# Modulation sums in their own banks, a distance table sent by another queue, and multiplications with constants in TensorE's gaps

## The reference

```python
# layer 1
mod = silu(c) @ w_ada + b_ada
shift, scale, gate = split(mod, 3)
h = rms_norm(x, norm_gain) * (1 + scale) + shift
proj = h @ w_in                 # kc, vc, z, gate, k, v, q of two attentions
...                             # a banded attention and one over compressed, selected and windowed keys,
                                # each with a bias that depends on the distance of query and key
x = x + gate * (concat(o_a * silu(z_a), o_b * silu(z_b)) @ w_out)
# layers 2 and 3, i = 0, 1
mod = silu(c2) @ ada_w[i] + ada_b[i]           # six vectors of 1024
a = rmsnorm(h, norm1[i]) * (1 + sc1) + sh1
y = diff_attention(a, ctx, ...) if i == 0 else short_conv(a, ...)
h = h + g1 * y
h = h + g2 * swiglu(rmsnorm(h, norm2[i]) * (1 + sc2) + sh2, w_gate_up[i], w_down[i])
```

## Time and profile before

| | before |
|---|---|
| median of 3 executions | 1742.04 us (1740.34 to 1745.28) |
| span of the profiled execution | 1739.3 us |
| time of the profiled execution beside it | none is given; the span stands for it, 2.7 us below the median |
| PE busy | 1672.8 us, 96% |
| DVE, ACT busy | 975.8 us (56%), 677.8 us (39%) |
| mean granted clock of PE | 0.979 of full speed |

### The profile page before, as it was taken

How to read it: one execution, slowest core, us unless ns; L and a number is a source line. 1 busy time by engine, 2 the same in 40 slices (tenths; PEclk the granted TensorE clock), 3 DMA queues, 4 the chain that set the end, 5 groups by cost and what they waited for, 6 DMA issues and landing times.

```text
span 1739.3 us, 22898 instructions
## 1 busy us (share of the span) xinstructions
PE 1672.8 (96%) x8888; PEld 1393.1 (80%) x8888; DVE 975.8 (56%) x1805; ACT 677.8 (39%) x1413; POOL 61.9 (4%) x120
## 2 busy tenths in 40 slices
PE   4999999999999999999999999999999899999999
PEld 2777777777999999777888888887888788888887
DVE  4667466766777766767555554436555533333332
ACT  3334555564455555554322222223222433333221
POOL 0000000000000000000000000000000000000000
PEclk9899998999999999998999999998999999999999
DMA  8886333313223131222666665442443233333332
GB/s 309 210 244 180 99 96 98 97 25 87 54 55 104 38 110 37 86 73 56 189 179 182 192 178 153 116 122 75 130 124 97 73 97 97 97 97 97 100 113 79
DMA packets 290215, 202.02 MB, mean 116 GB/s; under 512 B 76247, under 2 KB 272072, under 8 KB 289082
## 3 DMA queue, kind: packets, MB, share of 16 engines
q1 hardware_dynamic: 266942, 133.21, 27.5%
q0 software_dynamic: 15536, 56.37, 10.7%
q10 hardware_dynamic: 7628, 10.97, 1.9%
HBM read 197.33 MB, written 5.28 MB: 116 GB/s over the span
## 4 chain that ended last, share of the span: by engine, by line
PE 88%; DVE 6%; ACT 2%; issue 2%; DMA 2%; ACTq 1%; SPq 0%; DVEq 0%
PE PS L864 13%; PE PS L866 13%; PE PS L865 13%; PE PS L848 4%; PE PS L846 4%; PE PS L847 4%; PE PS L1285 3%; PE PS L1287 3%; PE PS L1286 3%; PE PS L1335 2%; PE PS L1094 2%; PE PS L1359 2%; PE PS L1068 2%; PE PS L1347 1%; PE PS L1076 1%
## 5 line engine op out<-in xcount | busy, mean ns | idle before, releaser
L2016 DVE TENSOR_TENSOR WL<-WS,WH 128x512 fp32r<-128x512 f32 x416 | 268.0, 686 | 256.2 <-ACT WH L1508 255.7
L1508 ACT ACTIVATE WH<-WS 128x512 fp32r<-128x512 f32 x416 | 237.7, 621 | 179.1 <-PE PS L848 130.7
L864 PE MATMUL PS<-A3H,WL 128*128 128x512 f32 x672 | 262.9, 391 | 0.1
L866 PE MATMUL PS<-A3H,WH 128*128 128x512 f32 x672 | 261.7, 389 | 0.0
L865 PE MATMUL PS<-A3L,WH 128*128 128x512 f32 x672 | 261.4, 389 | 0.0
L864 PEld LDWEIGHTS PS<-A3H,WL 128*128 128x128 f32 x672 | 126.1, 188 | 30.0 <-issue 4.4
L866 PEld LDWEIGHTS PS<-A3H,WH 128*128 128x128 f32 x672 | 126.1, 188 | 26.4
L865 PEld LDWEIGHTS PS<-A3L,WH 128*128 128x128 f32 x672 | 126.2, 188 | 26.0
L846 PE MATMUL PS<-GH,WL 128*128 128x512 f32 x352 | 137.4, 390 | 0.6 <-DVE WL L2016 0.6
L848 PE MATMUL PS<-GH,WH 128*128 128x512 f32 x352 | 137.0, 389 | 0.0
L847 PE MATMUL PS<-GL,WH 128*128 128x512 f32 x352 | 137.0, 389 | 0.0
(11 more groups left out here) (363 smaller groups left out, 3429.1 us busy)
## 6 DMA issues: line engine op xcount, KB each, us to landing
AW<-in_ada_w POOLq DMA_DIRECT2D x96, 512.0 KB, 4.1
WS<-in_ffn_w_gate_up SPq DMA_DIRECT2D x88, 512.0 KB, 4.6
WS<-in_ffn_w_down SPq DMA_DIRECT2D x32, 512.0 KB, 4.2
WS<-in_sc_w_in SPq DMA_DIRECT2D x24, 512.0 KB, 4.1
AB<-in_w_ada SPq DMA_DIRECT2D x8, 1024.0 KB, 15.7
WS<-in_w_in SPq DMA_DIRECT2D x32, 256.0 KB, 4.4
WS<-in_diff_w_qkv SPq DMA_DIRECT2D x64, 128.0 KB, 2.6
WS<-in_ffn_w_down SPq DMA_DIRECT2D x16, 384.0 KB, 3.5
```

Source lines behind the costliest of these rows:

```text
L864: mm(PS[:, b, :], wl[:, k, :], hi[:, k, 0:S], start=(k == 0), stop=False)
L866: m = mm(PS[:, b, :], wh[:, k, :], hi[:, k, 0:S], start=False, stop=(k == KT - 1))
L1508: f(weights(p)[0][:, k, :], WS[:, p % 2, k, :], ACT.Copy).then_inc(w_hi, 1)
L2016: tt(lo[:, k, :], WS[:, p % 2, k, :], hi[:, k, :].bitcast(F32), ALU.subtract).then_inc(w_lo, 1)
```

## The change

Seven edits.

1. The two modulation sums of the launch go to banks 4 and 5 instead of `SMALL`, so they no longer wait for ACT's Ln; DVE reads them by a semaphore of their own.
2. The two DMAs of the distance table are issued by SP, behind `W2` and ahead of z0, with SP's own wait for `distance_rows`.
3. Seven matmuls of the identity with 512 columns of constants, into the unused bank 6, stand ahead of the modulation sums, and three behind them (`keep_busy`).
4. Every column sum multiplies by 128 columns of ones where it had one; the results lie 48 columns apart, and DVE reads them with that step.
5. `keep_busy(4, 6)` behind the sum of squares of the norms d and f.
6. `keep_busy(1, 6)` behind the sums at norm e.
7. `MW` for the first inner product is sent behind z4 instead of behind z5.

```diff
@@ SP
+            sp.wait_ge(rows_out, 16)
+            for head, at, n in ((0, 3 * P - 1, 2 * P), (8, P - 1, S)):
+                sp.dma_start(dist_table[head:head + 8, :, 0:n],
+                             bass.AP(dist_rows.tensor, head * 640 + at, [[640, 8], [-1, P], [1, n]]))\
+                    .then_inc(dist_out, 16)
...
             for j in range(8):
                 head_pair(a, j, (ZB if j >= 4 else ZA) * P + j % 4 * HD)
-                if j >= 5:
+                if j == 4:
+                    hidden_in(0)
+                if j > 5:
                     hidden_in(j - 5)
@@ PE
+            def keep_busy(n, bank):
+
+                for _ in range(n):
+                    mm(PS[:, bank, :], IDENT, CN[:, 0:S], start=True, stop=True)
+
+            def column_sums(bank, sums):
+
+                for f in range(KT):
+                    m = mm(bank[:, SUM_STEP * f:SUM_STEP * f + P], sums[:, f * P:(f + 1) * P], ONES, start=True, stop=True)
+                return m
+
             def add_up(a, u, sums):
 
-                bank = take_small(a, u)
-                for f in range(KT):
-                    m = mm(bank[:, f:f + 1], sums[:, f * P:(f + 1) * P], ONES[:, 0:1], start=True, stop=True)
-                m.then_inc(small_done, 1)
-                return m
+                column_sums(take_small(a, u), sums).then_inc(small_done, 1)
...
-            a = At("ada_a")
-            take_small(a, 0)
+            keep_busy(7, 6)
             for half in range(2):
                 pe.wait_ge(ada_used, 2 * KT - 2 + half)
-                for f in range(KT):
-                    m = mm(PS[:, SMALL, KT * half + f:KT * half + f + 1], AA[:, half, f * P:(f + 1) * P], ONES[:, 0:1],
-                           start=True, stop=True)
-            m.then_inc(small_done, 1)
+                m = column_sums(PS[:, 4 + half, :], AA[:, half, :])
+            m.then_inc(ada_sum, 1)
+            keep_busy(3, 6)
...
             def ffn(l, count, base):
                 square_sum("norm_d" if l == 0 else "norm_f", count, 2 if l == 0 else 1)
+                keep_busy(4, 6)
...
             add_beside(At("ada7b"), 0, 11, 5)
+            keep_busy(1, 6)
@@ ACT
-            act.wait_ge(rows_out, 16)
-            for head, at, n in ((0, 3 * P - 1, 2 * P), (8, P - 1, S)):
-                act.dma_start(dist_table[head:head + 8, :, 0:n],
...
@@ DVE
-                tt(cut(dst, at, 4), bank[:, 0:4], cut(VT, v, 4), ALU.add).then_inc(read, 1)
+                tt(cut(dst, at, 4), view(bank, [SUM_STEP, 4]), cut(VT, v, 4), ALU.add).then_inc(read, 1)
...
-            dve.wait_ge(small_done, At("ada_a").small(0) + 1)
-            tt(M1[:, 0:16], PS[:, SMALL, 0:16], VT[:, V_BADA:V_BADA + 16], ALU.add).then_inc(small_free, 1)
-            dve.wait_ge(small_free, At("ada_a").small(0) + 1)
+            dve.wait_ge(ada_sum, 1)
+            for half in range(2):
+                c = slice(KT * half, KT * half + KT)
+                m = tt(M1[:, c], view(PS[:, 4 + half, :], [SUM_STEP, KT]), VT[:, V_BADA + KT * half:V_BADA + KT * half + KT], ALU.add)
+            m.then_inc(ada_read, 1)
+            dve.wait_ge(ada_read, 1)
```

More of the change, by code:

```diff
@@ L51 @@
     ("norm_a", 1, 0, 0, 1, 0),
-    ("ada_a", 1, 0, 0, 1, 0),
+    ("ada_a", 1, 0, 0, 0, 0),
     ("kcvc", 1, 2, 2, 0, 0),
@@ L149, in pieces_by @@
     return sum(Z_PIECES[:k])
+SUM_STEP = 48
 GROUPS = 4
@@ L472, in hybrid_then_diff_conv @@
         ada_loaded = [sem(f"ada_loaded{k}") for k in range(KT)]
-        ada_used = sem("ada_used")
+        ada_used, ada_sum, ada_read = sem("ada_used"), sem("ada_sum"), sem("ada_read")
         part_in = [sem(f"part_in{s}") for s in range(A_SLOTS)]
@@ L790, in _ @@
             pool.wait_ge(cs_ready, 1)
-            pool.wait_ge(small_free, At("ada_a").small(0) + 1)
+            pool.wait_ge(ada_read, 1)
             pool.wait_ge(rows_out, 16)
@@ L909, in add_beside @@
                 pe.wait_ge(part_sum, sums_before(n + 1))
-                for f in range(KT):
-                    m = mm(PS[:, bank, f:f + 1], AA[:, n % 2, f * P:(f + 1) * P], ONES[:, 0:1], start=True, stop=True)
-                m.then_inc(small_done, 1)
+                column_sums(PS[:, bank, :], AA[:, n % 2, :]).then_inc(small_done, 1)
             def square_sum(stage, count, beside=0):
@@ L1582, in _ @@
             act.dma_start(dist_rows, US[:, :]).then_inc(rows_out, 16)
-            act.wait_ge(rows_out, 16)
-            for head, at, n in ((0, 3 * P - 1, 2 * P), (8, P - 1, S)):
-                act.dma_start(dist_table[head:head + 8, :, 0:n],
-                              bass.AP(dist_rows.tensor, head * 640 + at, [[640, 8], [-1, P], [1, n]]))\
-                    .then_inc(dist_out, 16)
             load_set(LN_AND_EXP)
@@ L2060, in take_part @@
                 bank = PS[:, SIDE if a.stage == "att" else SMALL, :]
-                tt(cut(dst, at, 4), bank[:, 0:4], cut(VT, v, 4), ALU.add).then_inc(read, 1)
-                tt(cut(dst, at + 4, 4), bank[:, 4:8], cut(VT, v + 4, 4), ALU.add).then_inc(small_free, 1)
+                tt(cut(dst, at, 4), view(bank, [SUM_STEP, 4]), cut(VT, v, 4), ALU.add).then_inc(read, 1)
+                tt(cut(dst, at + 4, 4), view(bank[:, 4 * SUM_STEP:], [SUM_STEP, 4]), cut(VT, v + 4, 4), ALU.add).then_inc(small_free, 1)
             def add_ada():
@@ L2494, in take_layer_part @@
                 c = 8 * (n - 1)
-                tt(M2[:, c:c + 8], PS[:, bank, 0:8], VT[:, V_ADAB + c:V_ADAB + c + 8], ALU.add).then_inc(part_read, 1)
+                tt(M2[:, c:c + 8], view(PS[:, bank, :], [SUM_STEP, 8]), VT[:, V_ADAB + c:V_ADAB + c + 8], ALU.add).then_inc(part_read, 1)
                 dve.wait_ge(part_read, n + 1)
```

## The result

The changed kernel takes 1726.22 us (median of 6 runs, 1722.76 to 1728.56) beside 1742.70 us for the kernel before (6 runs, 1736.94 to 1745.28). The ratio is 0.9905, with a 95% interval of 0.989 to 0.9919. So it is faster, by 14 to 19 us; the prediction said a gain of 13.4 us and a time of 1728.6 us.

A forecast was written before the change was run, and what follows sets the result against it. PE, busy 96% of 1739.3 us, bounds the kernel, losing time to half-clock stretches and few waits. Launch 1.7 + attention 6 + norms 6.6 - wider passes 0.9 = 13.4 us: 1742.0 becomes 1728.6 us, range 1718 to 1737.

The forecast's parts named there:

- Launch, up to the pair: Launch to pair kcvc: sums start at 38.5 to 39, first tile at 43, pair ends at 56.3, 8.5 us earlier.
- z0: First z panel: table ahead in SP's queue delays landing to 62.5, start to 65.2; half clock behind loses 2.4 us.
- `MW`: First inner product: weights sent one panel earlier remove PE's wait and the low clock behind it, 4.1 us gained.
- The launch in sum: All launch terms together: -2.4 + 4.1 = 1.7 us gained, between -1.3 and 11.6.
- The attention: Layer 1's attention: wide column sums remove four half-clock stretches, gaining 6 us, between 2 and 8.3.
- The norms: Norms d, e and f: wide sums and filling matmuls remove half-clock stretches, gaining 6.6 us, between 3.5 and 7.3.
- Rival B: Attention and norms: sums' width does not hold the clock; gains become 1 and 4.5; 1735.7 us; chance 0.21.
- Rival A: Launch: the table holds z0 little or not; launch gains 7 to 11.6, 1719 to 1723 us; chance 0.18.
- C: Launch: table delays z0 far more than 3 us, kernel slower; 1748 us if z0 lands at 82; chance 0.03.

## Why the prediction was right

**Launch, up to the pair.** The sums began at 38.98 (predicted 38.5 to 39), took 3.84 us for 32 passes (3.6), and the pair ran at full clock and ended at 57.5 (56.3). The first tile's first operation came at 43.36 (43), and PE began it at 45.80 (45.3). DVE's list was as late as forecast.

**z0.** Predicted: landing 62.5, start 65.2, clock low for some 5 us. Measured: 61.07, 63.70, and some ten matmuls at 0.43 us, 2.0 us lost. The mechanism was right, and the landing came 1.4 us earlier: z0 itself costs 0.6 us (1.4 gained at its start, 2.0 lost behind it) and not 2.4. One detail failed: the prediction let z0's packets wait on the DMA engines, while a good part of the time its issue was still held on SP (8.89 us). And the order alone isn't enough: with the table on ACT's queue PE still waited 3.6 us, and the cut by heads, in the same order, brought z0's landing forward by 4.5 us. Both count: where the transfer of 8 heads moved 332 packets in 2 us, that of 16 moved 528, and z0, which needs the same engines, lands behind it.

**`MW`.** Predicted 4.1 us; undoing it cost 3.1, with overlapping intervals. A wait of 0.9 us was left, since its transfer took 8.00 us to land among the late panels and not 4.1.

The launch in sum: 1.7 us predicted, 2.4 seen between the traces, 4.4 (2.4 to 6.1) when its edits are timed alone. Its lower bound of -1.3 was too high by the prediction's own terms: it takes the 4.1 us of `MW` as certain, though the floor given for `MW` is nothing.

**The attention.** This is the term that was furthest off: 6 us predicted, between 2 and 8.3, less 0.9 for the wider passes of all thirteen sums; 8.4 between the traces, after that cost. About 1.6 of the 8.4 are luck. They are the stretch at 336 to 340 of before, which the prediction left out of its sum and which the profiled execution of after lacks: the kernel with wide sums alone has it, at 330 to 334, and takes 61.3 us from g1 to h0 where after takes 59.7. That kernel gained 7.0 us up to norm b, nearly all of it in the attention, and this is the better measure of what the sums gave. The prediction held back because the work there is thin and a shift might bring another fall; that was right, since seven of the eleven traces with wide sums have one. The wider passes cost 0.1 us a sum.

**The norms.** 6.6 predicted; 5.7 between the traces (2.0 at d, 1.9 at e, 1.8 at f; predicted 2.3, 1.9, 2.4), 5.4 when undone. The 1.9 at e is partly luck too, since the clock fell there in three other traces with the same code.

Rival B, that the width isn't what holds the clock, is out by two kernels, the wide sums alone and the narrow ones put back. Rival A was wrong for this kernel, though a table that doesn't hold z0 gave 1720.8 us with GpSimd, within the 1719 to 1723 that A was worked out to. C came nowhere near.

## What to carry to other kernels

Look at the granted clock in short stretches and at what ran just ahead: in this kernel a run of matmuls with one column often cost the clock although the engine was busy all the time, and the same sums over 128 columns took 0.1 us more and kept it. A large transfer between places in DRAM is worth cutting so that its outer dimension has 16 parts (97.6% of the engines' time and not 50.9%), and belongs on a queue in which nothing urgent stands behind it, for later transfers and the issuing engine both wait. A gain ahead of a transfer that sets the next start is worth next to nothing while that transfer stays where it is. Whether the filling at the launch pays once the table no longer holds z0 was not run. Last, one profile is one execution: stretches at the half clock come and go between executions of kernels with the same code at that place, 1.6 us each in the attention, so a term is better read from several traces than from one pair.

## What was not expected of the hardware

An issue behind two large transfers in the same queue took 12.55 us of ACT's own time, where 0.6 us are usual, and it halted the engine's computing, although about half of the table had yet to move when it ended. Two transfers of 8 heads kept 82% of the DMA engines busy by the software queue and 51% by a hardware queue. And the clock at norm e fell in four traces with wide sums and not in seven others, of kernels that differ there by one matmul or by nothing.
